# A two-layer attention and MLP trunk: rotary exchange by ScalarE copies, three norms' sums on GpSimd, another order of the first residual pair

## The chip, the cores and the metric

The kernel runs on one core of one Trainium2 chip. The metric is the device time of one execution in microseconds. Engines are named as in the profile: PE is TensorE, DVE is VectorE, ACT is ScalarE, POOL is GpSimd, and SP issues DMAs.

## The reference

Two layers work on x (512 tokens, 1024 channels, fp32). Each has a token-mixing part and an MLP, both with an RMS norm on the way in and on the way out:

```python
h = rms_norm(x, g_mix_pre); proj = h @ w_in          # latents, band q/k/v, stick q/k/v, gates
o_a = mla_branch(...) @ w_o_mla                      # causal, 8 heads, partly rotary
o_b = swa_branch(...) @ w_o_swa                      # band of 128, rotary on the full head of 64
o_c = stick_breaking_branch(...) @ w_o_sb
mixed = gates[0] * o_a + gates[1] * o_b + gates[2] * o_c
x = x + rms_norm(mixed @ w_out, g_mix_post)          # POST
h = rms_norm(x, g_mlp_pre)                           # MPRE
x = x + rms_norm(square(relu(h @ w_up)) @ w_down, g_mlp_post)   # MPOST
# rms_norm(x, g) = x * rsqrt(mean(x*x) + eps) * g
# rope: [x1*cos - x2*sin, x2*cos + x1*sin] on the two halves x1, x2 of a head
```

## The kernel before

Channels lie on the 128 partitions and tokens in the free dimension, so a tile is 128 channels by 512 tokens. Every fp32 product is done as three products of a high and a low part (`_hi`, `_lo`). ScalarE makes the high part with a copy, and VectorE makes the low part with a subtraction. Weights stream in chunks of 512 KB through a ring of four. Each engine has its own program in one written order, and semaphores tie them.

A norm's mean over channels is a sum over the 8 tiles and over the 128 partitions. ScalarE squares each tile (`square`, L1044) and VectorE adds the squares into `acc` (`gather`, L1582 and L1586). Then `norm_sum` on TensorE multiplies by a matrix of ones, which sums over partitions and gives every partition the sum. For POST and MPOST the last square is not added by VectorE: a second product adds it in PSUM. ScalarE then makes a first guess of the reciprocal root by Ln and Exp (`norm_guess`, L1047 and L1049), and VectorE refines it (`norm_refine`, L1599, L1589, L1592).

The last tiles of `out` and of the last `down` group (tiles 5, 6, 7) are computed in two halves of 256 tokens (`halved`). So the norm of the first half can be finished while TensorE works on the second half. Behind it `residual` (L1617 scales, L1626 adds to x) works on pairs of tiles, then h_hi (L1063) and h_lo (L1605) follow. Those are the next stage's operands, and that stage (`three_halves`) takes them up tile by tile, first half first: `up` group 0 after POST, the next layer's latents after MPOST. The sums of the second half stand inside `three_halves` behind its first tile. At the end of the second layer nothing follows but the residual and the stores. MPRE is not needed before `up` group 1, because its factor is applied later.

The band branch rotates one key tile and four query tiles per layer. `rope` on ScalarE writes a high part (L1140), `rope_in` on VectorE the low part (L1740, L1743) and the cos product (L1748). `rotate` on TensorE exchanges the halves of each head by a product with the matrix SWAP (L779, L780). `rope_turn` on VectorE does the sin product (L1755) and the sum (L1758). In VectorE's order `rope_in(2)` stands ahead of the maximum of the first band head and `rope_in(3)` ahead of that of the second. Each maximum goes to GpSimd (`band_maximum`, L2279) and then to TensorE (`band_shift`, L569).

GpSimd's program in one layer is: two memsets, 8 reductions of maxima (L2302), two memsets, 8 more reductions (L2279), then elementwise products (L2321) and additions into `mix` (L2290).

Of the kernel before, what the change touches and what calls it, by code (L numbers as in the profile page):

```python
# [12 lines left out]
P = 128  # L13
# [8 lines left out]
KT = D // P  # L22
# [100 lines left out]
IDENT, SWAP, NEG_TRI, NEG_ONE, ONE, MASK_CAUSAL, MASK_PREV, MASK_STRICT, NEG_PART, TRI01 = range(10)  # L123
N_CONST = 10 * P
# [25 lines left out]
SUMS_PRIOR = (0, 5, 6)  # L150
# [13 lines left out]
def trunk(nc, A_x, A_pos, A_w, A_vec, A_const, A_first, out):  # L164
    x_spill = nc.dram_tensor("x_spill", (P, KT, SEQ), F32).ap()
    now = [0]
    with ExitStack() as ctx:
# [23 lines left out]
        cst = place("cst", [P, 9, P], F32R)  # L191
# [88 lines left out]
        rsq = place("rsq", [P, SEQ], F32, r3 + 14336)  # L280
        hf = place("hf", [P, 3, SEQ], F32, r3 + 16384)
# [7 lines left out]
        rp_hi = place("rp_hi", [P, SEQ], F32R, r1 + 16384 + 10240)  # L289
        rp_lo = place("rp_lo", [P, SEQ], F32R, r1 + 16384 + 12288)  # L290
# [10 lines left out]
        pv_bank, rot_bank, norm_bank = bank[6], bank[7], bank[7]  # L301
# [37 lines left out]
        sum_all = signal("sum_all", 8)  # L339
# [27 lines left out]
        rp_h = signal("rope_in_hi", 5)  # L367
        rp_l = signal("rope_in_lo", 5)
        rot = signal("rotated", 5)
# [81 lines left out]
        def sum_bank(h):  # L451
            return pv_bank if h else norm_bank
# [65 lines left out]
        with nc.Block() as block:  # L518
# [38 lines left out]
            def _(pe):  # L557
# [23 lines left out]
                def norm_sum(j, h=0):  # L581
                    e, cols = square_of(j, KT - 1, h)
                    if j == MPRE:
                        pe.wait_ge(*summed(SUMMED_AT[j] + gathered(j, e)))
                        column_sums(sum_bank(h), [acc[:, :]]).then_inc(sum_all.sem, 1)
                        return
                    pe.wait_ge(*summed(SUMMED_AT[j] + gathered(j, e - 1)))
                    pe.matmul(sum_bank(h)[:, cols], cst[:, ONE, :].bitcast(F32), acc[:, cols], start=True, stop=False)
                    pe.wait_ge(*squared(SQUARED_AT[j] + e + 1))
                    pe.matmul(sum_bank(h)[:, cols], cst[:, ONE, :].bitcast(F32), sq[:, e % 2, cols], start=False, stop=True)\  # L590
                      .then_inc(sum_all.sem, 1)

# [30 lines left out]
                def halved(name, hi, lo, j, ready=None):  # L623

                    for t, h, one in tiles_of(*name):
                        tile(one, hi, lo, ready if t == 0 else None,
                             (lambda: norm_sum(j)) if (t, h) == (HALF, 1) else None, cols_of(t, h))

                def three_halves(names, ready, j):


                    def piece(name, t, h):
                        cols = HALVES[h]
                        return three(tile_bank(name)[:, cols],
                                     [(weight(C[name], t), (h_hi[:, t, cols], h_lo[:, t, cols]))],
                                     start=t == 0 and h == 0, last=t == KT - 1)

                    for name in names:
                        pe.wait_ge(*wlo(C[name] + 1))
                        take_bank(name)  # L640
                    for h in range(2):
                        for t in range(KT):
                            pe.wait_ge(*hlo(ready + KT * h + t + 1))
                            for name in names:
                                mm = piece(name, t, h)
                                if h and t == KT - 1:
                                    mm.then_inc(full.sem, 1)
                            if (t, h) == (0, 0):
                                layer = now[0]
                                now[0] = layer - (j == MPOST)  # L650
                                norm_sum(j, 1)
                                now[0] = layer
# [122 lines left out]
                def rotate(n):  # L775
                    pe.wait_ge(*rp_l(n + 1))
                    if n:
                        pe.wait_ge(*rot_used(n))
                    pe.matmul(rot_bank[:, :], cst[:, SWAP, :], rp_hi[:, :], start=True, stop=False)  # L779
                    pe.matmul(rot_bank[:, :], cst[:, SWAP, :], rp_lo[:, :], start=False, stop=True)\  # L780
                      .then_inc(rot.sem, 1)

# [94 lines left out]
                def up(g):  # L877
                    if g == 0:
                        three_halves([("up", 0, t) for t in range(3)], 2 * KT, POST)
                    for t in range(0 if g else 3, KT):  # L880
                        if g == 1 and t == 3:
                            norm_sum(MPRE)
                        tile(("up", g, t), h_hi, h_lo)

                def down(g):
                    if g + 1 == GROUPS:
                        halved(("down", g), u_hi[g % 2], u_lo[g % 2], MPOST, (u_l, KT * g))
# [11 lines left out]
                for now[0] in range(DEPTH):  # L899
                    if now[0]:  # L900
                        three_halves([("latent", i) for i in range(3)], 0, MPOST)
                    else:
                        three_tiles([("latent", i) for i in range(3)])
# [15 lines left out]
                    for h in range(HEADS):  # L919
# [8 lines left out]
                        if h + 3 < HEADS:  # L928
                            tile(("gate", 0, h + 3), h_hi, h_lo, None, between)
                        elif h == HEADS - 3:  # L930
                            tile(("swa_k",), h_hi, h_lo, None, between)
                        elif h == HEADS - 2:
                            tile(("swa_vt",), h_hi, h_lo, None, between)
                            rotate(0)

                    turn(("swa_v",), ("swa_vt",), vt_at(None))
                    rotate(1)
                    tile(("swa_q", 1), h_hi, h_lo)
                    band_scores(0)
                    rotate(2)  # L940
# [4 lines left out]
                    for t in range(PAIRS):  # L945
# [7 lines left out]
                        if t < 2:  # L953
                            rotate(t + 3)
# [52 lines left out]
                    halved(("out",), mix_hi, mix_lo, POST, (mix_l, 0))  # L1007
# [6 lines left out]
                    if now[0] + 1 == DEPTH:  # L1014
                        norm_sum(MPOST, 1)

            @block.scalar
            def _(act):
# [16 lines left out]
                def square(j, t, src, h=0):  # L1035
                    e, cols = square_of(j, t, h)
                    if e == 0 and (j or now[0]):
                        act.wait_ge(*summed(SUMMED_AT[j]))
                        act.wait_ge(*sum_all(SUMS_PRIOR[j]))
                    elif e == KT + 1:  # L1040
                        act.wait_ge(*sum_all(SUM_OF[j, 0] + 1))
                    elif e > 1:
                        act.wait_ge(*summed(SUMMED_AT[j] + gathered(j, max(1, e - 2))))
# [92 lines left out]
                def rope(n, name, scale):  # L1136
                    tile_ready(name)
                    if n:
                        act.wait_ge(*rot(n))
                    act.activation(rp_hi[:, :], tile_bank(name)[:, :], ACT.Copy, scale=scale).then_inc(rp_h.sem, 1)  # L1140
# [143 lines left out]
                act.activation(cst[:, :, :], cst_f[:, 0:9 * P].rearrange("p (a c) -> p a c", a=9), ACT.Copy)\  # L1284
# [241 lines left out]
            def _(dve):  # L1526
# [46 lines left out]
                def gather(j, t, h=0):  # L1573
# [5 lines left out]
                    if t == 1:  # L1579
                        if j or now[0]:  # L1580
                            dve.wait_ge(*sum_all(SUMS_PRIOR[j]))
# [14 lines left out]
                def norm_refine(j, h=0):  # L1596
# [4 lines left out]
                    newton(n, sum_bank(h)[:, cols], D, rs0[:, cols], rst[:, cols], rstd[:, cols])  # L1601
# [7 lines left out]
                def residual(p, h, n0, then):  # L1609
# [125 lines left out]
                def rope_in(n, name, scale):  # L1735
                    dve.wait_ge(*rp_h(n + 1))
                    if n:
                        dve.wait_ge(*rot(n))
                    if scale == 1.0:
                        dve.tensor_tensor(rp_lo[:, :], tile_bank(name)[:, :], rp_hi[:, :].bitcast(F32), ALU.subtract)\  # L1740
                           .then_inc(rp_l.sem, 1)
                    else:
                        dve.scalar_tensor_tensor(out=rp_lo[:, :], in0=tile_bank(name)[:, :], scalar=scale,  # L1743
                                                 in1=rp_hi[:, :].bitcast(F32), op0=ALU.mult, op1=ALU.subtract)\
                           .then_inc(rp_l.sem, 1)
# [5 lines left out]
                def rope_turn(n, name, dst, hi):  # L1751
                    dve.wait_ge(*rot(n + 1))
                    if n:
                        dve.wait_ge(*rp_sum(n))
                    dve.tensor_tensor(rb[:, :], rot_bank[:, :], sin_r, ALU.mult).then_inc(rot_used.sem, 1)  # L1755
# [515 lines left out]
            def _(pool):  # L2271
# [19 lines left out]

                for now[0] in range(DEPTH):
# [31 lines left out]
                    for t in range(KT):  # L2324
                        mix_in(2, t)


def constants():

    p, c = np.arange(P)[:, None], np.arange(P)[None, :]  # L2330
    swap = np.where(p % HEAD < HEAD // 2, p + HEAD // 2, p - HEAD // 2)
    mats = [p == c, swap == c, -(p >= c).astype(np.float32), -np.ones((P, P)), np.ones((P, P)),
# [95 lines left out]
```

## Time and profile before

| | us |
|---|---|
| median of 3 runs (1742.21 to 1742.78) | 1742.46 |
| the profiled execution | 1742.36 |
| its span, first to last instruction | 1740.5 |
| PE busy | 1714.0 |
| DVE busy | 1089.4 |
| ACT busy | 852.8 |
| POOL busy | 141.9 |

The mean granted clock of TensorE is 0.997. Busy time of PE counts overlapping products once, so it is not PE at its peak: products of 512 columns are recorded as 0.39 us but start some 0.23 apart, those of 256 columns as 0.28 and start 0.12 apart. A row of a timeline begins with its start and its length in us. Behind it, in brackets, stands the idle time of its engine and what ended it. Neighbouring equal instructions are merged, with their count.

### The profile page before, as it was taken

Reading aid. Unit: us, or ns where it says so; the run is one execution under the profiler, and the core shown is the slowest. Engines: PE = TensorE matmul, PEld = TensorE weight load, DVE = VectorE, ACT = ScalarE, POOL = GpSimd, SP = SyncE. Lnnn points to the kernel's source line nnn. Section 1 sums busy time; section 2 is a strip of 40 time slices with the busy share of each in tenths; the row PEclk is TensorE's granted clock in tenths of the full one; section 3 lists DMA queues with packets and bytes.
Section 4 is the critical chain, followed back from the end, with each engine's and each line's share of the span. In section 5 each row is a group of like instructions: output and inputs, shape, how many; then the busy total and the mean of one; then the engine's idle time right before and its main releaser. Section 6 shows DMA issues by size and latency. Waiting matters only on the chain.

```text
span 1740.5 us, 21889 instructions
## 1 busy us (share of the span) xinstructions
PE 1714.0 (98%) x8633; PEld 1445.9 (83%) x8633; DVE 1089.4 (63%) x1498; ACT 852.8 (49%) x1203; POOL 141.9 (8%) x140
## 2 busy tenths in 40 slices
PE   8999999999999999999999999999999999999997
PEld 6888888888898888888888888888888988888886
DVE  8887877665557534364597777867655665343545
ACT  7576666665445414131466755766544453232223
POOL 0111211111200000000001111111111000000000
PEclk9999999999999999999999999999999999999999
DMA  4121112122332222222321211122224222222222
GB/s 149 67 77 61 60 68 69 67 72 85 124 131 73 97 97 97 97 98 97 116 85 64 76 61 61 61 73 73 73 85 156 75 98 97 97 97 97 97 97 73
DMA packets 47496, 152.10 MB, mean 87 GB/s; under 512 B 5153, under 2 KB 9633, under 8 KB 47394
## 3 DMA queue, kind: packets, MB, share of 16 engines
q1 hardware_dynamic: 45664, 147.42, 24.5%
q10 hardware_dynamic: 1730, 3.28, 0.5%
q8 instruction: 69, 1.13, 0.3%
q14 instruction: 33, 0.27, 0.0%
HBM read 146.49 MB, written 4.19 MB: 87 GB/s over the span
## 4 chain that ended last, share of the span: by engine, by line
PE 83%; issue 7%; DVE 6%; ACT 3%; POOL 1%; DMA 0%; DVEq 0%; ACTq 0%; SPq 0%; POOLq 0%
PE bank L564 77%; PE bank L569 3%; PE bank L822 1%; PE bank L873 1%; POOL mix L2290 1%; ACT w_hi L1027 1%; DVE w_lo L1570 0%; DMA x<-in_x 0%; DVE h_lo L1605 0%; DVE hf L1617 0%; PE bank L573 0%; PE bank L672 0%; DVE x L1626 0%; DVE fb L1816 0%; ACT dn L1084 0%
## 5 line engine op out<-in xcount | busy, mean ns | idle before, releaser
L564 PE MATMUL bank<-h_hi,w_hi 128*128 128x512 f32 (+1 forms) x1224 | 477.7, 390 | 5.0 <-DVE h_lo L1605 2.8
L564 PE MATMUL bank<-h_hi,w_lo 128*128 128x512 f32 (+1 forms) x1224 | 472.3, 386 | 0.0
L564 PE MATMUL bank<-h_lo,w_hi 128*128 128x512 f32 (+1 forms) x1224 | 472.2, 386 | 0.0
L1027 ACT ACTIVATE w_hi<-raw 128x1024 fp32r<-128x1024 f32 (+2 forms) x269 | 271.1, 1013 | 219.7 <-DMA raw<-in_w 219.2
L1570 DVE TENSOR_TENSOR w_lo<-raw,w_hi 128x1024 fp32r<-128x1024 f32 (+2 forms) x269 | 317.0, 1182 | 63.9 <-ACT w_hi L1027 57.2
L564 PEld LDWEIGHTS bank<-h_hi,w_hi 128*128 128x128 f32 x1224 | 230.5, 188 | 55.0 <-issue 5.5
L564 PEld LDWEIGHTS bank<-h_hi,w_lo 128*128 128x128 f32 x1224 | 230.2, 188 | 47.0
L564 PEld LDWEIGHTS bank<-h_lo,w_hi 128*128 128x128 f32 x1224 | 230.6, 188 | 45.1 <-issue 1.7
L564 PE MATMUL bank<-u_hi,w_hi 128*128 128x512 f32 (+1 forms) x560 | 208.0, 371 | 0.0
L564 PE MATMUL bank<-u_hi,w_lo 128*128 128x512 f32 (+1 forms) x560 | 207.7, 371 | 0.0
L564 PE MATMUL bank<-u_lo,w_hi 128*128 128x512 f32 (+1 forms) x560 | 207.7, 371 | 0.0
L564 PEld LDWEIGHTS bank<-u_hi,w_hi 128*128 128x128 f32 x560 | 105.5, 188 | 18.3
L564 PEld LDWEIGHTS bank<-u_hi,w_lo 128*128 128x128 f32 x560 | 105.5, 188 | 18.2
L564 PEld LDWEIGHTS bank<-u_lo,w_hi 128*128 128x128 f32 x560 | 105.5, 188 | 18.0
L1890 DVE TENSOR_TENSOR usq<-relu 128x512 f32<-128x512 f32 x64 | 44.2, 691 | 104.0 <-ACT relu L1231 103.5
L1231 ACT ACTIVATE relu<-bank 128x512 f32<-128x512 f32 x48 | 28.6, 595 | 139.1 <-PE bank L564 139.1
L1908 DVE TENSOR_TENSOR y<-bank,y 128x512 f32<-128x512 f32 x32 | 22.1, 692 | 98.7 <-PE bank L564 98.7
L564 PE MATMUL bank<-o_hi,w_hi 128*128 128x512 f32 x192 | 76.6, 399 | 0.0
L564 PE MATMUL bank<-o_hi,w_lo 128*128 128x512 f32 x192 | 75.0, 391 | 0.0
L1233 ACT ACTIVATE u_hi<-relu 128x512 fp32r<-128x512 f32 x64 | 40.5, 633 | 70.2 <-DVE relu L1885 68.7
L564 PE MATMUL bank<-o_lo,w_hi 128*128 128x512 f32 x192 | 74.8, 389 | 0.0
L2290 POOL TENSOR_TENSOR mix<-mix,gate 128x512 f32<-128x512 f32 x32 | 44.4, 1390 | 364.5 <-DVE gate L1865 364.5
(266 smaller groups left out, 2745.9 us busy)
## 6 DMA issues: line engine op xcount, KB each, us to landing
raw<-in_w SPq DMA_DIRECT2D x251, 512.0 KB, 3.2
x<-in_x SPq DMA_DIRECT2D x16, 256.0 KB, 3.3
side_raw<-in_w SPq DMA_DIRECT2D x6, 512.0 KB, 5.0
x_spill<-x ACTq DMA_DIRECT2D x8, 256.0 KB, 2.2
x<-x_spill SPq DMA_DIRECT2D x8, 256.0 KB, 3.2
out_y<-x SPq DMA_DIRECT2D x8, 256.0 KB, 2.1
raw<-in_w SPq DMA_DIRECT2D x8, 192.0 KB, 2.4
raw<-in_w SPq DMA_DIRECT2D x8, 128.0 KB, 2.3
```

The costliest lines, as they stand in the source:

```text
L564: mm = pe.matmul(o, s, m, start=start and i == 0 and j == 0, stop=last and i == n - 1 and j == 2, skip_group_check=True)
L569: return pe.matmul(o, stationary, moving, start=False, stop=True, skip_group_check=True)
L822: mm = pe.matmul(to[:, off + col:off + col + w], a, m, start=off + col == 0 and i == 0, stop=i == 2, skip_group_check=True)
L873: mm = pe.matmul(pv_bank[:, q0:q0 + w], v[:, j, h % 2, :], part[:, s], start=i == 0 and part is p_hi, stop=part is p_lo, skip_group_check= ...
L1027: act.activation(chunk_in(gc, w_hi, side_hi)[:, 0:w], chunk_in(gc, raw, side_raw)[:, 0:w], ACT.Copy)\
L1231: act.activation(relu[:, n % 2, :], tile_bank(name)[:, :], ACT.Relu).then_inc(free_of(name), 1)
L1233: act.activation(u_hi[g % 2][:, t, :], relu[:, n % 2, :], ACT.Square).then_inc(u_h.sem, 1)
L1570: dve.tensor_tensor(chunk_in(gc, w_lo, side_lo)[:, 0:w], chunk_in(gc, raw, side_raw)[:, 0:w], chunk_in(gc, w_hi, side_hi)[:, 0:w].bitcast( ...
L1890: dve.tensor_tensor(usq[:, n % 2, :], relu[:, n % 2, :], relu[:, n % 2, :], ALU.mult)\
L1908: ins = dve.tensor_tensor(y[:, t, :], tile_bank(name)[:, :], y[:, t, :], ALU.add)
L2290: pool.tensor_tensor(mix[:, t, :], mix[:, t, :], gated_at(b, t), ALU.add).then_inc(mix_add.sem, 1)
```

## The change

- **Rotary exchange.** `rope` issues four ScalarE copies of 32 partitions each, from PSUM into `rp`, with the halves of each head exchanged. The products with SWAP, the high and low parts for them and the matrix itself go. VectorE's cos product waits for all four copies, and its sin product reads `rp`.
- **Sums.** The norms POST, MPRE and MPOST are summed over partitions by `norm_total` on GpSimd. For POST and MPOST it first adds the last square to `acc`, then reduces over partitions into `total`, for each half. Guess and refinement read `total` in SBUF. The sums of x and of the latents stay on TensorE.
- **Residual.** The first pair is scaled and added before the second is scaled.

```diff
-                def norm_sum(j, h=0):
-                    e, cols = square_of(j, KT - 1, h)
-                    if j == MPRE:
-                        pe.wait_ge(*summed(SUMMED_AT[j] + gathered(j, e)))
-                        column_sums(sum_bank(h), [acc[:, :]]).then_inc(sum_all.sem, 1)
-                        return
...
+                def norm_total(j, h=0):
+                    e, cols = square_of(j, KT - 1, h)
+                    pool.wait_ge(*rs_step(2 * SUM_OF[j, 0]))
+                    if j == MPRE:
+                        pool.wait_ge(*summed(SUMMED_AT[j] + gathered(j, e)))
+                    else:
+                        pool.wait_ge(*summed(SUMMED_AT[j] + gathered(j, e - 1)))
+                        pool.wait_ge(*squared(SQUARED_AT[j] + e + 1))
+                        pool.tensor_tensor(acc[:, cols], acc[:, cols], sq[:, e % 2, cols], ALU.add)\
+                            .then_inc(last_added.sem, 1)
+                        pool.wait_ge(*last_of(j, h))
+                    pool.partition_all_reduce(total[:, cols], acc[:, cols], P, bass.bass_isa.ReduceOp.add)\
+                        .then_inc(norm_all.sem, 1)
...
                     for t in range(KT):
                         mix_in(2, t)
+                    norm_total(POST)
+                    norm_total(POST, 1)
+                    norm_total(MPRE)
+                    norm_total(MPOST)
+                    norm_total(MPOST, 1)
...
                 def norm_guess(j, h=0):
                     n, cols = SUM_OF[j, h], ALL if j == MPRE else HALVES[h]
-                    act.wait_ge(*sum_all(n + 1))
-                    guess(2 * n, rs0[:, cols], sum_bank(h)[:, cols], 0.0, 1.0 / D)
+                    act.wait_ge(*norm_all(n - 2))
+                    guess(2 * n, rs0[:, cols], total[:, cols], 0.0, 1.0 / D)
...
                 def rope(n, name, scale):
                     tile_ready(name)
-                    if n:
-                        act.wait_ge(*rot(n))
-                    act.activation(rp_hi[:, :], tile_bank(name)[:, :], ACT.Copy, scale=scale).then_inc(rp_h.sem, 1)
+                    if n > 1 or now[0]:
+                        act.wait_ge(*rot_used(n - 1))
+                    for q in range(4):
+                        to, of_ = (slice(g * HEAD // 2, (g + 1) * HEAD // 2) for g in (q, q ^ 1))
+                        act.activation(rp[n % 2][to, :], tile_bank(name)[of_, :], ACT.Copy, scale=scale).then_inc(rot.sem, 1)
...
                 def rope_in(n, name, scale):
-                    dve.wait_ge(*rp_h(n + 1))
...
+                    dve.wait_ge(*rot(4 * n + 4))
                     if n:
                         dve.wait_ge(*rpo_l(n))
                     dve.scalar_tensor_tensor(out=ra[:, :], in0=tile_bank(name)[:, :], scalar=scale, in1=cos_r,
                                              op0=ALU.mult, op1=ALU.mult).then_inc(free_of(name), 1)
...
                     if p == 0:
                         scaled_pair(0)
+                        added_pair(0)
                         scaled_pair(1)
-                        added_pair(0)
                         return
```

The calls of `norm_sum` and `rotate` on TensorE go with them. The waits on earlier sums name the new semaphores. The constant has nine matrices instead of ten.

## Rows read from the trace of the kernel before

**Rows 1.** The page: busy time of each engine (part 1), the chain (part 4).

```profile
PE 1714.0 (98%) x8633; PEld 1445.9 (83%) x8633; DVE 1089.4 (63%) x1498; ACT 852.8 (49%) x1203; POOL 141.9 (8%) x140
...
PE 83%; issue 7%; DVE 6%; ACT 3%; POOL 1%; DMA 0%; DVEq 0%; ACTq 0%; SPq 0%; POOLq 0%
```

**Rows 2.** Sum products by line, then two pieces of the chain (start, us).

```profile
L588 PE MATMUL bank<-acc,cst x16: 377/380/483, 507.1 to 1729.4; 128*128 128x256 f32 x16
...
35.27 1.72 PE bank L573 x4
...
1720.34 0.43 PE bank L588 x2
```

**Rows 3.** Timeline of TensorE at one rotation (start, us, instruction).

```profile
147.27 0.39 PE L779 MATMUL bank<-rp_hi,cst 128*128 128x512 f32 x1
...
147.73 0.39 PE L564 MATMUL bank<-h_hi,w_hi 128*128 128x512 f32 x1
```

**Rows 4.** GpSimd instructions by line (ns: min/median/max), then its timeline.

```profile
L2321 POOL TENSOR_TENSOR fb<-fb,tri x64: 455/464/1454, 247.5 to 1246.1; 128x128 f32<-128x128 f32 x64
L2321 POOLq MODIFY_POOL_CONFIG  x4: 87/88/88, 233.2 to 1093.3; - x4
...
L2290 POOL TENSOR_TENSOR mix<-mix,gate x32: 1285/1294/1747, 288.5 to 1330.8; 128x512 f32<-128x512 f32 x32
...
L2279 POOL PARTITION_ALL_REDUCE bmxr<-bmx x16: 1782/1783/1784, 168.3 to 1091.5; - x16
...
231.51 1.78 POOL L2279 PARTITION_ALL_REDUCE bmxr<-bmx  x1 [0.98 <-DVE bmx L1680]
...
247.48 2.58 POOL L2321 TENSOR_TENSOR fb<-fb,tri 128x128 f32<-128x128 f32 x6 [14.18 <-DVE fb L1816]
```

**Rows 5.** Timeline of ScalarE: neighbouring copies from PSUM, merged.

```profile
27.85 1.58 ACT L1294 ACTIVATE cf<-bank 128x512 f32<-128x512 f32 x3
...
118.04 1.20 ACT L1126 ACTIVATE mk_hi<-bank 64x512 fp32r<-64x512 f32 x2
```

**Rows 6.** Timelines of four engines in the banded stage, first layer.

```profile
164.36 0.58 ACT L1140 ACTIVATE rp_hi<-bank 128x512 fp32r<-128x512 f32 x1
...
173.24 0.68 DVE L1748 SCALAR_TENSOR_TENSOR ra<-bank,cf 128x512 f32<-128x512 f32 x1
...
175.93 1.78 POOL L2279 PARTITION_ALL_REDUCE bmxr<-bmx  x1 [5.88 <-DVE bmx L1680]
...
177.76 0.68 PE L569 MATMUL bank<-bmxr,cst 128*128 128x256 f32 x4
```

**Rows 7.** Timelines from attention to MLP, first layer.

```profile
505.86 0.38 ACT L1044 ACTIVATE sq<-bank 128x256 f32<-128x256 f32 x1 [1.18 <-PE bank L564]
...
508.17 0.38 ACT L1047 ACTIVATE rs<-bank 128x256 f32<-128x256 f32 x1 [1.56 <-PE bank L590]
...
518.28 0.41 DVE L1599 TENSOR_TENSOR rst<-rs 128x256 f32<-128x256 f32 x1
...
522.91 0.48 DVE L1605 SCALAR_TENSOR_TENSOR h_lo<-x,vec_all,h_hi 128x256 fp32r<-128x256 f32 x1
...
524.66 0.28 PE L564 MATMUL bank<-h_hi,side_hi 128*128 128x256 f32 x1
```

**Rows 8.** Timelines from MLP to the second layer.

```profile
870.78 0.40 ACT L1044 ACTIVATE sq<-y 128x256 f32<-128x256 f32 x1
...
879.33 0.28 PE L564 MATMUL bank<-h_hi,side_hi 128*128 128x256 f32 x1
```

**Rows 9.** Timeline of ScalarE at the end.

```profile
1729.44 0.42 ACT L1044 ACTIVATE sq<-y 128x256 f32<-128x256 f32 x1 [0.43 <-DVE y L1920]
...
1730.64 0.38 ACT L1047 ACTIVATE rs<-bank 128x256 f32<-128x256 f32 x1 [0.39 <-PE bank L590]
```

**Rows 10.** Stretch near the start: us, busy times, clock, DMA share, GB/s.

```profile
11.00:16.00 5.00, 4.39 (x12) 3.49 (x13) 4.76 (x9) 5.00 (x9) 0.00 (x0) 0.66 0.93 374
```

**Rows 11.** VectorE's rotated sum by line (ns: min/median/max).

```profile
L1758 DVE TENSOR_TENSOR ra<-ra,rb x10: 691/692/1049, 149.8 to 1061.2; 128x512 f32<-128x512 f32 x10
```

More of the change, by code:

```diff
@@ L121 @@
 VECS = V_SINK + HEADS
-IDENT, SWAP, NEG_TRI, NEG_ONE, ONE, MASK_CAUSAL, MASK_PREV, MASK_STRICT, NEG_PART, TRI01 = range(10)
-N_CONST = 10 * P
+IDENT, NEG_TRI, NEG_ONE, ONE, MASK_CAUSAL, MASK_PREV, MASK_STRICT, NEG_PART, TRI01 = range(9)
+N_CONST = 9 * P
 TRIG = 4 * 4
@@ L288, in trunk @@
         rb = place("rb", [P, SEQ], F32, r1 + 16384 + 8192)
-        rp_hi = place("rp_hi", [P, SEQ], F32R, r1 + 16384 + 10240)
-        rp_lo = place("rp_lo", [P, SEQ], F32R, r1 + 16384 + 12288)
+        rp = [place(f"rp{i}", [P, SEQ], F32, r1 + 16384 + 10240 + 2048 * i) for i in range(2)]
         later_f = place("later_f", [P, 768], F32, r1 + 24576)
@@ L300, in trunk @@
         proj, score = bank[0:2], bank[2:5]
[L301 removed]
+        pv_bank, norm_bank = bank[6], bank[7]
         side_bank = bank[3]
@@ L338, in trunk @@
         summed = signal("summed", 2 * (SQUARES - 2) + KT)
-        sum_all = signal("sum_all", 8)
+        sum_all = signal("sum_all", 3)
+        last_added = signal("last_square_added", 4)
+        norm_all = signal("norm_summed", 5)
         rs_guess = signal("rs_guess", 16)
@@ L366, in trunk @@
         trig_r = signal("trig_scaled", 2)
-        rp_h = signal("rope_in_hi", 5)
-        rp_l = signal("rope_in_lo", 5)
-        rot = signal("rotated", 5)
+        rot = signal("rope_turned", 20)
         rot_used = signal("rot_used", 5)
@@ L449, in gathered, with last_of @@
             return 0 if e == 0 else e + 1 if e < KT - 1 or j == MPRE else e
-        def sum_bank(h):
-            return pv_bank if h else norm_bank
+        def last_of(j, h):
+            return last_added(2 * (j == MPOST) + h + 1)
         def slot(name):
@@ L621, in tile, with halved, three_halves @@
                     mm.then_inc(full.sem, 1)
-                def halved(name, hi, lo, j, ready=None):
+                def halved(name, hi, lo, ready=None):
                     for t, h, one in tiles_of(*name):
-                        tile(one, hi, lo, ready if t == 0 else None,
-                             (lambda: norm_sum(j)) if (t, h) == (HALF, 1) else None, cols_of(t, h))
-                def three_halves(names, ready, j):
+                        tile(one, hi, lo, ready if t == 0 else None, None, cols_of(t, h))
+                def three_halves(names, ready):
                     def piece(name, t, h):
@@ L647, in three_halves @@
                                     mm.then_inc(full.sem, 1)
[L648 to L652, printed above, removed]
                 def three_tiles(names):
@@ L878, in up @@
                     if g == 0:
-                        three_halves([("up", 0, t) for t in range(3)], 2 * KT, POST)
+                        three_halves([("up", 0, t) for t in range(3)], 2 * KT)
                     for t in range(0 if g else 3, KT):
-                        if g == 1 and t == 3:
-                            norm_sum(MPRE)
                         tile(("up", g, t), h_hi, h_lo)
@@ L900, in _ @@
                     if now[0]:
-                        three_halves([("latent", i) for i in range(3)], 0, MPOST)
+                        three_halves([("latent", i) for i in range(3)], 0)
                     else:
@@ L1005, in _ @@
                         out_tile(2, t + 1)
-                    halved(("out",), mix_hi, mix_lo, POST, (mix_l, 0))
+                    halved(("out",), mix_hi, mix_lo, (mix_l, 0))
                     up(0)
```

51 lines of the change are left out of this document (11 added, 40 removed).

## The prediction

> **What bounds the kernel now.** I read the page first: busy shares and the chain that ended last [rows 1]. The reader is to see that TensorE is busy for 98% of the span and carries 83% of the chain, with 7% "issue" besides, which is mostly the same engine. So a product taken away is worth its own pace, if nothing else then comes late. Second, the products that go [rows 2, 3]. Third, the kinds of GpSimd instruction, because the sums are put there, and what stands between two kinds [rows 4]. Fourth, ScalarE, VectorE and GpSimd around the rotary tiles [rows 5, 6]. Last, the three places where layers and halves meet, because there TensorE's next operand hangs on a norm [rows 7 to 9].
>
> **Products removed.** A sum over 256 columns is two fp32 products of 0.43 us each, 0.86 us [rows 2]: the second row has one product's pace, its two passes. Four such per layer (two halves, two norms) and one of 512 columns for the norm between the residuals, also 0.86 (two of 512 took 1.72). That is 2 x 5 x 0.86 = 8.6 us of TensorE. A rotation is two products, 147.27 to 147.73, 0.46 us [rows 3]; ten of them give 4.6 us. If nothing waited, 13.2 us would go.
>
> **The middle norm (MPRE).** Its reduction of 512 columns costs 1.78 us on GpSimd [rows 4], its kind follows a reduction, and its result is needed four tiles later. It hides behind the MLP's products. Gain 2 x 0.86 = 1.7 us.
>
> **The other two norms: a chain of GpSimd.** Each half now goes: square, GpSimd add, GpSimd reduction, ScalarE's Ln. The add of 256 columns lies between 0.46 us (128 columns) and 1.29 us (512) [rows 4]; linear, 0.74. The reduction of 256 columns is not in the trace; 512 took 1.78, the ends are 0.9 (half) and 1.8, and I take 1.0. Handing over between engines costs 0.05 to 0.1.
> Between the two kinds stands a third thing. MODIFY_POOL_CONFIG is recorded exactly where the queue passes from reductions to elementwise products and never between two of one kind [rows 4]. At present that is once in each direction per layer (L2302 has the like of the row shown), both in long waits. The new order is add, reduction, add, reduction, reduction, add, reduction, add, reduction, so one stands between each pair but the middle one. What a change of kind costs no row measures. From below it is the record's 0.09 us. From above it is the stretch from that record at 233.2 to the next elementwise product at 247.48, 14.1 us, though that product also waited for VectorE. Nothing in between is nearer to either end, so I take the middle, S = 7.1 us, and keep both ends.
> The Trainium skill (GPSIMD Engine Reference, 2.1 Instruction dispatch) says that the first call to freshly loaded GpSimd code pays about 6 us that no instruction shows. No run here shows that number yet; by it the sum below would be some 9 us lower, an estimate of 1798.
>
> *Attention to MLP, each layer* [rows 7]. The last square of the first half ends at 506.24, and Ln started at 508.17. New: 506.3 + 0.74 + 7.1 + 1.0 + 0.1 = 515.2, so 7.1 later, and the residual, h_hi and h_lo of this half with it. The second half's squares stand behind that Ln in ScalarE's order, so the last ends near 522.2; GpSimd has changed kind again by then (515.2 + 7.1 = 522.3). Add to 523.1, change to 530.2, reduction to 531.2, Ln 531.3. Exp and handover take 0.86, so VectorE's refinement starts at 532.2 instead of 518.28, 13.9 later. The next h_lo (522.91, ends 523.4) is then at 537.3, and 0.2 later by the new order of pairs: 537.5. TensorE took it up at 524.66, so it is 12.8 us late, and the 1.7 us of sums removed there are inside this. Two layers: +25.7.
> *MLP to next layer, once* [rows 8]. The same chain. Here the sum waited in TensorE's order and a weight split filled VectorE, so the first half is only some 7.4 later. The last square, 870.78 + 0.40, ends at 878.6; 0.1 + 0.74 + 7.1 + 1.0 + 0.05 gives Ln at 887.6; from Ln to the first h_lo's end 6.0 us as in rows 7 (0.86 + 4.63 + 0.48), and 0.2: 893.8. TensorE had it at 879.33: +14.4.
> *The end* [rows 9]. First half +7.4, square ends at 1729.86 + 7.4 + 0.1 = 1737.4, Ln at 1746.4 instead of 1730.64: +15.8. The order of pairs adds a dependent step here, +0.2. Together +16.0, all on the path.
> *TensorE's clock* [rows 10]. After a stop of 2.6 us near the start the granted clock was 0.66 over 5 us, that is 1.7 us of full clock lost. Each boundary now has stops of 6 us and more. One loss per boundary is exposed, since the others fall ahead of a further wait: 3 x 1.7 = +5.1 (0 to 10).
>
> **The order of residual pairs.** The second scaling used to fill VectorE while the first addition's operand settled. Now addition follows scaling directly: 0.69 long against a pace of 0.60, 0.1 to 0.2 us each time, and ScalarE's first copy could start 0.5 us earlier, but it was VectorE that carried this stretch. Priced inside the terms above.
>
> **Rotation by ScalarE.** One copy of 0.58 us becomes four. Two copies that move between partition ranges started 0.61 apart (1.20 for two), three on all partitions 0.50 apart (1.58 for three) [rows 5]. So four take 2.42 or 2.1 us; I take 2.42, as these move partitions too. VectorE's split (0.60) goes, and its cos product now waits for all four copies: 1.25 us later.
> Behind it in VectorE's order stands the band's maximum. *Rotation 2* starts on ScalarE at 164.36 without idling [rows 6], so cos product, maximum, and rotated sum come 1.3 later. *Rotation 3* stands behind that on ScalarE: the cos product at 173.24 moves to 175.2, the maximum with it, and GpSimd's reduction from 175.93 to 177.9. TensorE's subtraction at 177.76 followed the reduction's end (177.71) at once; it moves to 179.7, so TensorE loses 1.9 there and gets back the 0.5 of its rotation. *Rotation 4* adds 1.2 by the same steps and the last removed product gives 0.5 back, half of it lost to VectorE's order. Net +2.4 per layer, +4.8 (with 2.1 us for four copies: +1.0 per layer). The constant's ScalarE copy is 0.1 shorter, ahead of a wait: nothing.
> The last sum in VectorE's rotation took 1.05 us instead of 0.69 where GpSimd's reduction lay beside it [rows 11]. The Trainium skill (SBUF — State Buffer, "Who interferes with whom") says that a VectorE instruction with two SBUF inputs contends with a GpSimd one that reads SBUF, and the row agrees. By it the residual's sums beside the new GpSimd adds grow by up to 0.4 each, under 1 us per boundary; I leave it out of the sum and in the range.
>
> **Sum.** Profiled execution: 1742.36 us (span 1740.5 and 1.9 around it), 0.1 under the median 1742.46. It becomes 1742.4 + 25.7 + 14.4 + 16.0 + 5.1 + 4.8 - 1.7 = **1807**.
>
> **Rivals.**
> *A, a change of kind is nearly free* (0.1 us). For it: 0.09 us is all that is recorded. Against it: an instruction that appears only at changes should do something. Then each attention-to-MLP boundary gains 0.5 (VectorE's stream, not the products, bounds it), the layer boundary loses 0.5 and the end 2.2: 1742.4 + 4.8 - 1.7 - 1.1 + 0.5 + 2.2 = 1747.
> *B, faster:* one mechanism, TensorE alone decides. The chains through GpSimd and ScalarE would have to stay inside the slack that they have, which decides at S under about 0.5 us and four copies under 1 us together. Then 13.2 less 2.2 at the end remain: 1732. For it is only 98% busy; against it are chains without slack, as TensorE's subtraction 0.05 us behind GpSimd's end [rows 6].
> *C, a change of kind costs 10 to 14 us*, as when weights stream beside it. Two changes per boundary and at the end lie on the path, eight in all, so each microsecond of S is 8 us: at S = 10, 1742.4 + 64.3 + 23 = 1830; at 14, 1862.
> *D, the reduction doesn't shrink with columns* (1.8 instead of 1.0): eight on the path, +6.4, 1813. Inside the likeliest case's range.
>
> **Chances.** Forecast with D (S from 5.5 to 9): 0.74, its own range 1790 to 1825. C 0.15, A 0.08, B 0.03. Of A, half stays within 0.2% (3.5 us), about what a measurement of this kernel can tell from no change. So slower 0.93, same 0.04, faster 0.03. Range 1785 to 1838, which leaves out A, B and the upper part of C.
>
> **What would show it.** In the changed profile GpSimd's reduction starts about S + 0.1 after its add ends; if it follows within 0.2 us, A holds. Ln waits for it, and TensorE's longest waits are on h_lo at the three boundaries, with a clock under 1 behind them. At the end Ln to last addition is unchanged but starts 16 later. In the band stage cos products start 2.4 us after the first copy and TensorE reaches its second subtraction 1.9 later. Wrong altogether if those waits are under 2 us.

## The result, and the profile after

The changed kernel takes 1809.0 us (median of 4 runs, 1806.0 to 1810.1) against 1742.3 for the one before: ratio 1.038, 95% interval 1.0365 to 1.0397. The forecast was 1807, with a range of 1785 to 1838. The profiled execution took 1808.7 us with a span of 1806.9, which is 66.4 more than the span before.

The page of the changed kernel, busy times and then the chain that ended last; they answer to [rows 1].

```profile
PE 1717.8 (95%) x8577; PEld 1451.4 (80%) x8577; DVE 1089.2 (60%) x1488; ACT 871.0 (48%) x1233; POOL 173.3 (10%) x158
...
PE 78%; issue 9%; DVE 6%; ACT 4%; POOL 2%; DMA 0%; DVEq 0%; SPq 0%; POOLq 0%; ACTq 0%
```

TensorE has 56 instructions fewer and is busy 3.8 us longer: half clock ate more than the products that went. GpSimd's busy time grew by only 31 us, and 2% of the chain is on it. What it costs is not in its busy time. It is in the waits of the changed kernel (us in total, times, longest):

```profile
ACT rs L1012 <- POOL total L2261: 65.6, 8, 8.5
...
POOL total L2261 <- issue: 47.2, 8, 6.1
...
PE bank L564 <- DVE h_lo L1572: 41.0, 9, 9.3
...
PE bank L564 <- DVE ra L1706: 5.9, 4, 2.4
```

The second row is the one to learn to read: GpSimd stood 47.2 us before its reductions, eight times, and nothing that the profile shows released it. The timeline of GpSimd from attention to MLP has the same thing (start, us, instruction, idle before):

```profile
511.74 0.73 POOL L2258 TENSOR_TENSOR acc<-acc,sq 128x256 f32<-128x256 f32 x1 [33.96 <-ACT sq L1009]
518.33 1.81 POOL L2261 PARTITION_ALL_REDUCE total<-acc  x1 [5.86 <-issue]
528.08 1.24 POOL L2258 TENSOR_TENSOR acc<-acc,sq 128x256 f32<-128x256 f32 x1 [7.95 <-DVE acc L1553]
535.16 1.81 POOL L2261 PARTITION_ALL_REDUCE total<-acc  x1 [5.84 <-issue]
583.98 4.19 POOL L2261 PARTITION_ALL_REDUCE total<-acc  x1 [47.01 <-DVE acc L1553]
```

A reduction begins 5.86 us after the add of the other kind ends; the one that follows a reduction (583.98) waits for its data alone. The configurations recorded ahead of the ten reductions say the same, since 16 are two for each of the eight that follow an add:

```profile
L2261 POOLq MODIFY_POOL_CONFIG  x16: 4/10/13, 512.7 to 1789.3; - x16
```

The chain of waits shows that the configuration is recorded at once and that the stretch behind it is empty:

```profile
511.74 0.73 POOL acc L2258
512.47 0.19 issue
512.66 0.01 POOLq L2261
512.67 0.02 issue
512.70 0.01 POOLq L2261
512.71 5.62 issue
518.33 1.82 POOL total L2261
```

TensorE's timeline at the same place, the first products of the two halves, and then stretches of it (us, busy times of five engines, granted clock, DMA share, GB/s):

```profile
525.94 0.55 PE L564 MATMUL bank<-h_hi,side_hi 128*128 128x256 f32 x1 [6.16 <-DVE h_lo L1572]
```

```profile
520.00:526.00 6.00, 0.06 (x1) 0.09 (x1) 4.80 (x10) 3.57 (x10) 0.13 (x1) 0.66 0.27 87
526.00:532.00 6.00, 6.00 (x40) 6.00 (x41) 5.00 (x10) 1.88 (x5) 1.24 (x1) 0.77 0.02 4
532.00:540.00 8.00, 2.06 (x17) 1.86 (x16) 2.00 (x5) 1.63 (x4) 1.81 (x1) 0.94 0.00 0
540.00:546.00 6.00, 6.00 (x29) 6.00 (x30) 5.93 (x12) 3.67 (x7) 0.00 (x0) 0.51 0.00 0
546.00:552.00 6.00, 6.00 (x52) 6.00 (x51) 3.53 (x7) 0.91 (x2) 0.00 (x0) 1.00 0.01 3
```

TensorE stops for 6 us, works on the first half, stops again, and then runs 6 us at the lower of its two levels: 29 products where the next 6 us hold 52.

Where the 66.4 us lie follows from TensorE's position at the end of each stage (us, from its two timelines; for the halved tiles it is the start of the third-last product in both). In the kernel before, a first half's sum of 0.7 us, start to start, lies ahead of each `out` and `down` row; it is taken from there and counted to the boundary behind, as the forecast counts it:

```
end of                       before   after    shift   the stage's own       forecast
out products, layer 1        515.32   519.79    4.47   rotation 5.2           2.4
halved up tiles, layer 1     532.94   552.98   20.04   boundary 14.9          14.6
down products, layer 1       868.37   886.63   18.26   middle norm -1.1       -0.9
halved latent tiles          887.64   922.28   34.64   boundary 15.7          16.1
out products, layer 2       1375.35  1411.52   36.17   rotation 2.2           2.4
halved up tiles, layer 2    1392.97  1444.51   51.54   boundary 14.7          14.6
down products, layer 2      1728.40  1778.16   49.76   middle norm -1.1       -0.9
the span                    1740.5   1806.9    66.4    end 15.9               16.0
```

The boundaries and the end came out at the forecast's total; the rotation did not. ScalarE and VectorE in the banded stage of layer 1, and TensorE behind them, against [rows 6]:

```profile
164.76 2.43 ACT L1107 ACTIVATE rp<-bank 32x512 f32<-32x512 f32 x4
...
173.50 2.43 ACT L1107 ACTIVATE rp<-bank 32x512 f32<-32x512 f32 x4
```

```profile
170.45 1.41 DVE L1715 TENSOR_TENSOR ra<-ra,rb 128x512 f32<-128x512 f32 x1
...
175.96 0.69 DVE L1706 SCALAR_TENSOR_TENSOR ra<-bank,cf 128x512 f32<-128x512 f32 x1 [1.23 <-ACT rp L1107]
```

```profile
176.80 0.47 PE L564 MATMUL bank<-o_hi,w_hi 128*128 128x512 f32 x1 [2.41 <-DVE ra L1706]
```

Four copies take 2.43 us, as said. But TensorE stops before the `o` products, on the cos product, because that product is what releases the projection's PSUM bank. The second stop of the stage goes by another path. The fourth rotation's cos product waits for its copies, the band's denominators (`dn`) stand behind it in VectorE's order, and TensorE's next values need the bank that the scaled output (`of`) releases:

```profile
189.83 0.69 DVE L1706 SCALAR_TENSOR_TENSOR ra<-bank,cf 128x512 f32<-128x512 f32 x1 [3.61 <-ACT rp L1107]
190.56 0.69 DVE L1727 TENSOR_TENSOR dn<-bank,dn 64x512 f32<-64x512 f32 x1
...
192.61 0.68 DVE L1656 TENSOR_TENSOR of<-bank,dn 64x512 f32<-64x512 f32 x1 [0.23 <-ACT dn L1049]
...
193.44 0.36 PE L564 MATMUL bank<-bp_hi,wv_hi 128*128 128x256 f32 x1 [1.74 <-DVE of L1656]
```

The kernel before has the same chain and a stop of 0.51 us there.

### The profile page after: what moved, and what is told of

The parts are those of the page before. It is cut to its first block, busy times and chain, and to the rows that moved or that the text cites. A ratio compares the mean times of both kernels' runs of the same rounds, so it can differ in the third digit from the quotient of the medians.

```text
span 1806.9 us, 21835 instructions
## 1 busy us (share of the span) xinstructions
PE 1717.8 (95%) x8577; PEld 1451.4 (80%) x8577; DVE 1089.2 (60%) x1488; ACT 871.0 (48%) x1233; POOL 173.3 (10%) x158
## 3 DMA queue, kind: packets, MB, share of 16 engines
HBM read 146.42 MB, written 4.19 MB: 83 GB/s over the span
## 4 chain that ended last, share of the span: by engine, by line
PE 78%; issue 9%; DVE 6%; ACT 4%; POOL 2%; DMA 0%; DVEq 0%; SPq 0%; POOLq 0%; ACTq 0%
PE bank L564 72%; PE bank L569 3%; PE bank L796 1%; ACT rp L1107 1%; POOL total L2261 1%; PE bank L847 1%; POOL mix L2247 1%; DVE hf L1584 1%; DVE w_lo L1537 1%; ACT w_hi L992 0%; POOL acc L2258 0%; DMA x<-in_x 0%; PE bank L654 0%; DVE fb L1773 0%; DVE h_lo L1572 0%
```

## Experiments

Each is compared with the kernel before, run beside it on the same chip (medians 1741.5 to 1741.7 there). First the three parts of the change, each alone.

**Rotation alone.** The hunks of the copies, `rp`, `rope_in`, `rope_turn` and SWAP, nothing else.

> Only the rotation part of the change: four copies by ScalarE and no swap product; the norms and the order of pairs as before. Theory 1: the trace after shows TensorE's position 5.3 us later across the banded stage of layer 1 and 2.3 us in layer 2, all from VectorE's cos product waiting for the fourth copy and releasing the bank late, with half clock behind two stops in layer 1 and one in layer 2. Alone it should be 1742.4 + 7.7 = 1750, or up to 1.6 more if layer 2 gets the second clock loss too (1749 to 1752). Theory 2: the excess over the forecast's 4.8 us came from the sums' stops and is absent here: 1745 to 1747.

1751.65 us (1748.51 to 1752.48), ratio 1.0055 (1.0042 to 1.0067), so 10.1 us. At the upper end of theory 1. The stops are those of the whole kernel (2.41 and 1.73 us in layer 1). Layer 1 has half clock behind its second one only, layer 2 behind both. A stretch behind the second stop of each layer:

```profile
188.00:194.00 6.00, 4.27 (x33) 3.58 (x30) 4.54 (x8) 3.38 (x5) 0.00 (x0) 0.79 0.10 39
...
1058.00:1064.00 6.00, 5.86 (x25) 5.24 (x26) 3.97 (x9) 1.28 (x3) 2.29 (x2) 0.72 0.01 3
```

**Sums alone.** The hunks of `norm_total`, `total` and the waits; rotation by products.

> Only the partition sums on GpSimd; rotation and order of pairs as before. Theory 1: the parts add. From the trace after: three boundaries 14.7, 15.5 and 14.6, end 15.7, less 1.7 of the middle norm, 58.7 us in all, so 1801 (1799 to 1803). Theory 2: rotation and sums share a cover and don't add: more than 3 us off 1801.

1797.2 us (1796.9 to 1798.2), ratio 1.0322 (1.0308 to 1.0336): 55.7 us, 3 less than expected and outside theory 1's range, though the reason of theory 2 does not hold. Parts alone sum to 65.8 against 66.7 for the whole (1809.0 less 1742.3), so they add within 1 us. It is the split between them that moves. One piece of it is seen: behind the second stop of layer 2's banded stage the whole kernel runs at full clock, the rotation alone at 0.72 (the row above). This is the whole kernel:

```profile
1084.00:1090.00 6.00, 4.26 (x34) 3.77 (x31) 5.25 (x10) 2.76 (x6) 1.35 (x1) 1.00 0.01 3
```

The profiled executions show where the rest of the 3 us lies. 1.4 us come before anything that the change moves: the first product that reads the latents starts at 46.57 us here, at 47.94 in the whole kernel and at 47.75 in the kernel before. Another 0.8 us come from the latents of layer 2. From the last halved tile to that product TensorE needs 19.17 us in both kernels with the sums and 19.94 without them, and the table above books this gain under the rotation of layer 2 (2.2, which is 3.0 without it). The boundaries and the end are 60.5 us here against 61.2.

**Order of pairs alone.**

```
-                        scaled_pair(1)
                         added_pair(0)
+                        scaled_pair(1)
```

> Only the order of the first residual pair. Theory 1 (as in the forecast): VectorE's stream carries these stretches, the order adds a dependent step of 0.1 to 0.2 us at each boundary and at the end, so between 0 and +1 us: 1742.4 to 1743.4. Theory 2: ScalarE's first copy 0.5 us earlier is what TensorE waits for, at the layer boundary above all: 0.5 to 2 us faster, 1740.5 to 1742.

1741.76 us, ratio 1.0002 (0.9993 to 1.0011). Nothing that can be told from zero.

Next, what in the sums costs.

**Reductions only.**

```
-                    if t == 0 or t == KT - 1 and j != MPRE:
+                    if t == 0:
                         return
...
-                        pool.tensor_tensor(acc[:, cols], acc[:, cols], sq[:, e % 2, cols], ALU.add)\
-                            .then_inc(last_added.sem, 1)
-                        pool.wait_ge(*last_of(j, h))
```

> The whole change, but VectorE adds the last square of each half as it adds the others, so GpSimd's queue holds reductions only and changes kind once per layer, in a long wait. Theory 1: what costs is the change of kind, 8 times 5.9 us between the add's end and the reduction's start. It goes, and with it some of the half clock; the adds shrink from 0.73 and 1.25 on GpSimd to 0.42 on VectorE. What stays is a reduction of 1.8 us in place of 0.78 through TensorE, about 2.5 us per boundary, and the rotation: 1757 (1750 to 1761), every reduction within 0.2 us of its add. Theory 2: the reduction itself starts some 6 us late whenever it follows a wait or new data, with no change of kind needed: 1804 to 1809.

1757.8 us (1754.2 to 1760.0), ratio 1.0094 (1.0079 to 1.011). The forecast of theory 1 to a microsecond. GpSimd's timeline, and what its reductions wait for:

```profile
510.62 1.81 POOL L2250 PARTITION_ALL_REDUCE total<-acc  x1 [34.47 <-DVE acc L1547]
521.94 2.08 POOL L2250 PARTITION_ALL_REDUCE total<-acc  x1 [9.51 <-DVE acc L1547]
```

```profile
POOL total L2250 <- DVE acc L1547: 782.1, 10, 291.5
```

VectorE's add ended at 510.41 (509.99 + 0.42), the reduction starts 0.2 later. The queue held elementwise additions before this one too, and the configuration for the reduction is recorded at 476.4, behind the last of them and 34 us before the reduction starts:

```profile
L2250 POOLq MODIFY_POOL_CONFIG  x4: 7/7/7, 476.4 to 1342.6; - x4
```

So the change was made in the wait. The experiment takes away GpSimd's add and the wait for its own result together; what ties the 5.9 us to the kind is the configuration, recorded ahead of each of the eight reductions that follow an add and of neither of the two that follow a reduction. That fits the kernel before, which never paid for it, although it changed kind once in each direction per layer. The 14.2 us in [rows 4], the upper bound, were then a wait for VectorE with the change hidden inside.

**First halves by VectorE.** As before, for h = 0 only.

> The whole change, but VectorE adds the last square of the first halves; GpSimd still adds that of the second halves. Four of the eight changes to a reduction leave the path, each with its add. Theory 1: every one of them was on the path for its full length, so half of what reductions only gave back (1809.0 - 1757.8 = 51.2) comes back, 25.6 us, a little more with the second change now starting earlier: 1783 (1778 to 1788). Theory 2: the second half's chain hides most of the first's, so the first halves' changes are nearly free: 1800 or more. Theory 3: the other way, 1770 or less.

1782.95 us (1781.9 to 1785.6), ratio 1.024 (1.0224 to 1.0256). Half the changes, half the price (26.1 of 51.2 us): the eight lie one behind the other, as the forecast had it. The wait on "issue" is 24.1 us in 4 times.

**Reductions by maximum.** `ReduceOp.max` for `ReduceOp.add` in the kernel with reductions only.

> As reductions only, but GpSimd's reductions for the norms take the maximum in place of the sum, so the norms are not the reference's. It measures what a reduction of 256 columns costs by its operation. Theory 1: time goes with columns, and a sum costs over twice a maximum (512 columns: 4.19 against 1.78 us): a maximum of 256 takes 0.9 us (0.8 to 1.0), the 1.0 of the forecast was right for a maximum and wrong for a sum; eight of them on the path give back 7 us: 1751. Theory 2: a floor of 1.8 us whatever the columns: 1.8 us again, 1758.

1753.05 us (1749.1 to 1753.6), 4.8 less than with sums. Lines of the two kernels (ns: min, median, max), first maximum, then sum:

```profile
L2250 POOL PARTITION_ALL_REDUCE total<-acc x10: 1062/1351/2746, 510.7 to 1740.2; - x10
```

```profile
L2250 POOL PARTITION_ALL_REDUCE total<-acc x10: 1792/2080/4198, 510.6 to 1742.7; - x10
```

A maximum of 256 columns takes 1.06 us alone and 1.35 beside VectorE; a sum 1.80 and 2.08. Theory 1 in its kind, somewhat less in its size: no floor, the sum costs 0.73 us more.

Then the rotation.

**One copy.**

```
-                    for q in range(4):
-                        to, of_ = (slice(g * HEAD // 2, (g + 1) * HEAD // 2) for g in (q, q ^ 1))
-                        act.activation(rp[n % 2][to, :], tile_bank(name)[of_, :], ACT.Copy, ...).then_inc(rot.sem, 1)
+                    act.activation(rp[n % 2][:, :], tile_bank(name)[:, :], ACT.Copy, ...).then_inc(rot.sem, 4)
```

> The rotation part alone, but with one ScalarE copy over all partitions in place of four over a quarter each, so the exchange between the quarters is left out of what is computed; everything else as in the rotation part. Theory 1: the length of the four copies (2.43 us against 0.58) is the whole cost, because it delays the cos product that releases the bank and the band's maximum behind it. With one copy the bank is released 0.6 us earlier than before, no stop comes, the ten pairs of products (4.6 us) are gained, and some of the 0.3 us waits: 1737 (1735 to 1739). Theory 2: rb read from SBUF beside GpSimd's reduction (1.41 against 1.05 us for the sum), or the loss of the split product's timing, costs by itself: 1741 or more.

1736.8 us (1735.7 to 1737.7), ratio 0.9973 (0.9962 to 0.9984). The ten pairs of products are worth what they were priced at (4.7 us) if nothing comes late. Everything that the rotation loses hangs on three more copies of 0.6 us: 14.9 us between this and the four copies.

**Two rotations copied**, 0 and 1; 2 to 4 by products.

> The kernel before, with rotations 0 and 1 by the four copies and rotations 2 to 4 by products as before. Theory 1: only rotations 3 and 4 stand on the path; the first two copies lie beside products, and in the trace after TensorE was 0.75 and 1.7 us ahead of the kernel before when it came to the third. So their two pairs of products are gained, 2 x 2 x 0.46 = 1.8 us less a few tenths: ratio 0.9990 to 0.9996. Theory 2: every group of four copies delays something behind it on ScalarE: ratio over 1.001.

1741.54 us, ratio 0.9999 (0.999 to 1.0008). No loss, so theory 2 falls; but no gain either that could be told from zero. What the products gave, a new wait took in part: TensorE's second rotary query tile waits for the cos product, whose bank it needs:

```profile
155.65 0.47 PE L566 MATMUL bank<-h_hi,w_hi 128*128 128x512 f32 x1 [0.54 <-DVE ra L1752]
```

**Reordered.** The same instructions of the rotation alone; in `scalar`, and likewise in `vector`:

```
-                    split(C["swa_q", 2] + 2)
...
                             rope(3, ("swa_q", 2), 0.125)
+                            split(C["swa_q", 2] + 2)
...
-                            rope(4, ("swa_q", 3), 0.125)
...
                         sink_exp(n + 1)
+                            rope(4, ("swa_q", 3), 0.125)
```

> The rotation part alone with the same instructions in another order: the copies of rotation 3 ahead of ScalarE's weight split, VectorE's cos product ahead of its own split, and rotation 4's copies and cos product behind the band's probabilities and denominators instead of ahead of them. Theory 1: TensorE's stop of 2.4 us comes from the bank that the cos product releases at 176.65; the split ahead of the copies is 1.04 us of it. The stop of 1.7 us at the values comes from rotation 4's copies ahead of the probabilities and goes entirely, with the half clock behind it. So of the +10.1 us of the rotation alone, some 2 x (1.0 + 1.7) + 2 x 1.6 = 8.6 us at most come back: ratio 0.999 to 1.003. Theory 2: the copies' total length on ScalarE counts wherever they stand: ratio 1.005 as for the rotation alone.

1754.4 us (1752.2 to 1756.8), ratio 1.0072 (1.006 to 1.0085). A miss of theory 1: at the median 2.8 us slower than the rotation alone, which it was to mend, though the two intervals overlap. Its waits say why nothing was gained:

```profile
PE bank L566 <- POOL bmxr L2255: 10.4, 4, 2.9
```

The stop at the bank shrank to 1.48 us and the one at the values from 1.73 to 0.23, which also shows that rotation 4's place ahead of the denominators made that stop. But the band's maximum stands behind the moved pieces in VectorE's order, and TensorE stopped at its reduction instead, 2.32 and 2.87 us in layer 1. Relieving one of two chains moved the stop to the other.

**Third rotation earlier.** Only rotation 3, and VectorE's maximum ahead of its split too.

> The rotation part alone, with rotation 3 only ahead: its copies before ScalarE's weight split (1.04 us), and VectorE's cos product and the band's maximum before VectorE's own split. Rotation 4 stays where the change has it. Theory 1: what the copies cost is the stop that they put on two chains, the bank's release and the band's maximum, and both come about 1.1 us earlier here. In the reordered kernel only the first was earlier (stop 1.48 instead of 2.41) and the maximum, behind the split, came 1.0 us later and made a stop of 2.32 of its own. So now the stop before the o products is 1.4 us and none follows at the reduction: 1.0 to 1.4 us gained in each layer against the rotation alone, 1751.65 - 2.4 = 1749 (1747.5 to 1750), ratio 1.0035 to 1.0050. Theory 2: the order of the splits matters to the weight ring, and what is gained is lost to a late weight: ratio 1.0055 or above.

1749.2 us (1748.5 to 1749.8), ratio 1.0045 (1.0031 to 1.0059). The time is as theory 1 said, the reason is not. The bank's stop is 1.50 us, but a stop of 1.61 at the reduction followed, since the reduction now ran beside VectorE's split and took 2.68 us instead of 1.78. Together 3.11 against 3.09 (2.41 and 0.68) in the rotation alone. The profiled execution has gained clock: over 140 to 215 us the granted clock is 1.00 here and 0.95 there, at the same busy time of TensorE (68.3 and 68.4 us), 387 products' records against 373. That the order brought this is not shown. The five runs of the rotation alone reach from 1748.5 to 1752.5 us, and the two fastest (1748.51 and 1749.15, mean clock 0.996 and 0.997) take what this kernel takes.

```profile
176.71 2.68 POOL L2256 PARTITION_ALL_REDUCE bmxr<-bmx  x1 [5.65 <-DVE bmx L1666]
```

```profile
140.00:215.00 75.00, 68.33 (x387) 56.28 (x386) 53.01 (x80) 47.80 (x74) 12.97 (x8) 1.00 0.17 57
```

Last, what is worth keeping.

**Middle sum alone.** The norm between the residuals on GpSimd, all else as before.

```
+                    pool.wait_ge(*summed(SUMMED_AT[MPRE] + gathered(MPRE, KT - 1)))
+                    pool.partition_all_reduce(total[:, :], acc[:, :], P, bass.bass_isa.ReduceOp.add)\
+                        .then_inc(sum_all.sem, 1)
```

> The kernel before, with only the middle norm's sum (512 columns) on GpSimd. Theory 1: its two products of 0.86 us in each layer go and the reduction hides behind the MLP, although it takes 4.19 us: 1.7 us faster, ratio 0.9990. Theory 2: the result comes too late for y times rsq or the squared activation, or the reduction beside VectorE costs it as much: ratio 1.000 or above.

1739.8 us (1738.8 to 1740.7), ratio 0.999 (0.9981 to 0.9999): 1.7 us faster.

**Both.** The middle sum and the two copied rotations.

> The two parts that did not lose time alone: the middle norm's sum on GpSimd and rotations 0 and 1 by copies. Theory 1: they add, 1.7 us and at most 0.6: ratio 0.9987 (0.9982 to 0.9992), faster than before and than the whole change. Theory 2: one takes the other's: ratio 0.999 to 1.000.

1739.8 us (1738.3 to 1741.0), ratio 0.9988 (0.998 to 0.9997). Faster than both kernels of this case, and no more than the middle sum by itself.

## Why the prediction was right, and where it was not

*Sum products removed, 8.6 us.* Right in kind. At the halves a sum stood for 0.7 us rather than 0.86, start to start.

*Middle norm, -1.7.* Right: -1.7 us alone. Its reduction took 4.19 us and not 1.78, as the row in [rows 4] is of a maximum; it hides all the same.

The total of 1807 for 1809 owes much to luck: S was the middle between 0.09 and 14.1 us, and what it had too much made up for what other sizes had too little.

*The chain of GpSimd, 56.1 us for three boundaries and the end without the clock.* The steps stand as forecast: add, change, reduction, Ln; eight changes on the path, one behind the other, shown by taking away eight and four of them; the change back to the add hidden behind the second half's squares, all but some 0.9 us at the two boundaries behind attention (VectorE's sum ended at 527.13, the add started at 528.08; whether the change was still running then or the queue's waits cost it is not shown). Three sizes were off, and they cancel. The change of kind is 5.75 to 6.06 us, mean 5.9, not 7.1: 8 x -1.2 = -9.6. The reduction of 256 columns is 1.81, not 1.0: 8 x 0.81 = +6.5. The four second adds, beside VectorE, took 1.15 to 1.30, not 0.74: +2.0. So rival D's size was the true one. With the clock below they come to +1.0, while the table has 61.2 for boundaries and end, where the forecast had 61.2 as well; the 1.0 between the two is not accounted for.
The Trainium skill (GPSIMD Engine Reference, 2.1 Instruction dispatch) puts the first call to freshly loaded code at about 6 us that no instruction shows. The trace agrees in size, with 5.9 and an empty "issue" of 5.62; that it is a load of code no run here shows. The estimate of 1798 by it was low because the reduction (6.5 us), the second adds (2.0), the clock (2.1) and the rotation (2.6) were all priced too low beside it.

*The clock, 5.1.* Mechanism right, size too small. The stretch behind the second stop ran at 0.51 for 6.0 us (2.9 us lost), 0.50 with 4.4 us busy (2.2), and 0.50 with 4.2 (2.1): 7.2 us.

*The rotation, 4.8.* This term was mis-sized, and the step that failed is "Rotation 3 [...] TensorE's subtraction [...] moves to 179.7". The times on VectorE moved nearly as said (cos product at 175.96, forecast 175.2; the 0.36 us of a rotated sum beside a reduction, and 0.4 of a later start, are the rest). But TensorE never came to that subtraction on time: 12 products ahead of it need the bank that the cos product releases, and the kernel before had 0.95 us of slack there (released 173.92, first of the 12 at 174.87). Now it is released at 176.65, and the first of the 12 starts 1.93 us later than before (176.80). That this is the 1.9 of the forecast is chance, since it came by another path. *Rotation 4* was +1.2 in size (TensorE stopped 1.74 us before the values instead of 0.51) but not "by the same steps": it went through the denominators and `of`, not through a maximum and a reduction. What the forecast left out is the clock behind these stops, which it had charged to the boundaries alone: in layer 1 of the whole kernel the 12 `o` products took 4.57 us instead of 2.99, and the stretch from 194 to 200 us ran at 0.72. With one copy in place of four TensorE never waits for `ra`, and 0.3 us at most for `of`. Expected 4.8; in the whole kernel 7.4 (8.2 without the gain in layer 2's latents), alone 10.1.

*The order of pairs.* Right: nothing.

*SBUF contention, left in the range.* Adds of GpSimd beside VectorE 1.24 against 0.73 without. VectorE's sum of the last pairs, 1.10 against 0.69, shows the other side. The Trainium skill (SBUF — State Buffer, "Who interferes with whom") says that a VectorE instruction with two SBUF inputs contends with a GpSimd one that reads SBUF, and the trace agrees. It came to some 2 us on GpSimd's side, which is the side that lay on the path.

Rival A (a change of kind nearly free) and rival C (10 to 14 us) are both excluded by the 47.2 us in eight waits. B needed a change under 0.5 us and four copies under 1 us together, and they took 5.9 and 2.43 (its sum also comes to 1731, not 1732). Left open: what decides whether a stop in the banded stage is followed by half clock, and why the start of an execution differs by over 1 us from kernel to kernel.

## What to carry to other kernels

Before work is moved to GpSimd, write down the kinds of its instructions in queue order. Each change of kind that has no longer wait for data to hide in is some 6 us on the path, and a vector engine that takes the odd instruction of the other kind costs 0.42. A copy that several others stand behind is to be priced at every consumer, what releases its PSUM bank first of all; shortening one of two chains moves the stop. And when an engine at 98% stops for 2 us and more, look at the granted clock behind the stop: part of the price is there.

## What the runs showed of the hardware that was not expected

- A change from an elementwise add to a reduction on GpSimd: 5.75 to 6.06 us in eight cases, with nothing recorded but configurations of 0.1 us or less. It runs while the queue waits for data, and vanishes there (0.2 us from VectorE's add to the reduction after a wait of 34 us).
- The change back, from a reduction to an add, is bounded from above only: the earliest add started 7.48 us after the reduction's end (the sums alone), 0.6 after its data.
- A partition reduction's time depends on its operation: 256 columns 1.06 us as maximum and 1.80 as sum; 512 columns beside a busy VectorE 2.75 and 4.20.
- GpSimd's reductions stretch beside VectorE: a sum from 1.80 to 2.08, a maximum of 512 columns from 1.78 to 2.68.
- Four ScalarE copies of 32 partitions take 2.43 us, and each as long as one over 128 (0.59 against 0.58): the number of partitions saves nothing.
- The same stop of 2.41 us at the same place was followed by 12 products in 3.01 us, full clock, in the rotation alone, and in 4.57 us, 0.61, in the whole kernel (layer 1 in both). What decides between the two is not settled here.
